# One layer of a hybrid encoder on one core: the residual stage's output product in split passes, with its loads reordered and its transposes moved by one tile

## The reference, cut to what matters

```python
x = layer_norm(x, ln_in_g, ln_in_b)                      # trunk input, once
mix = sigmoid(g_a) * (y_a @ w_up_a) + sigmoid(g_b) * (y_b @ w_up_b)
x = layer_norm(ALPHA * x + (1 + gt1) * (mix @ w_out), ln1_g, ln1_b)
h2 = x * (1 + sc2) + sh2
ffn = hier_moe(h2, w_rg, b_rg, w_re, b_re, w_gate_e, w_up_e, w_down_e)
x = layer_norm(ALPHA * x + (1 + gt2) * ffn, ln2_g, ln2_b)
```

## Time and profile before

| what | value |
| --- | --- |
| median of 3 runs | 2190.09 us (2184.65 to 2190.78) |
| profiled execution, its own time | 2189.32 us |
| its span | 2187.5 us |
| TensorE busy | 1895.8 us, 87% of the span |
| VectorE, ScalarE, GpSimd busy | 949.9, 612.0, 435.6 us |
| mean granted TensorE clock | 0.922 of full speed |
| residual stage, first DMA issue to last instruction | 1600.2 to 1786.3 us, 186 us |

### The profile page before, as it was taken

How to read it: one execution, slowest core, us unless ns; L and a number is a source line. 1 busy time by engine, 2 the same in 40 slices (tenths; PEclk the granted TensorE clock), 3 DMA queues, 4 the chain that set the end, 5 groups by cost and what they waited for, 6 DMA issues and landing times. The chain is left out here.

```text
span 2187.5 us, 28807 instructions
## 1 busy us (share of the span) xinstructions
PE 1895.8 (87%) x10605; PEld 1495.8 (68%) x10606; DVE 949.9 (43%) x2110; ACT 612.0 (28%) x1257; POOL 435.6 (20%) x281
## 2 busy tenths in 40 slices
PE   7797998999999998979997699999977952999990
PEld 2597898989899898968883488888833531444440
DVE  5345756474665757234444111111125661333335
ACT  2543444435353443244443100100000000111114
POOL 0121112111212111111000121212115534222220
PEclk8798999999999999989997799999988975999995
DMA  9110110101011010132107611111052235688765
GB/s 355 53 63 18 35 55 28 57 23 53 32 53 55 20 55 13 34 114 72 36 8 272 238 34 53 38 44 34 24 194 87 87 153 193 218 290 262 217 163 178
DMA packets 61760, 219.24 MB, mean 100 GB/s; under 512 B 8430, under 2 KB 16846, under 8 KB 56534
## 3 DMA queue, kind: packets, MB, share of 16 engines
q1 hardware_dynamic: 53448, 190.03, 24.3%
q0 software_dynamic: 8208, 27.81, 5.2%
HBM read 177.90 MB, written 42.53 MB: 101 GB/s over the span
## 5 line engine op out<-in xcount | busy, mean ns | idle before, releaser
L143 PE MATMUL bk<-hT_high,w_high 128*128 128x352 f32 x840 | 302.4, 360 | 3.9 <-DVE ssq L1194 3.9
L144 PE MATMUL bk<-hT_low,w_high 128*128 128x352 f32 x840 | 278.9, 332 | 0.0
L145 PE MATMUL bk<-hT_high,w_low 128*128 128x352 f32 x840 | 278.4, 331 | 0.0
L2284 PE MATMUL psU<-wgu,xgT 128*128 x400 | 178.4, 599 | 2.0 <-DVE xgT L2350 2.0
L143 PEld LDWEIGHTS bk<-hT_high,w_high 128*128 128x128 f32 x840 | 166.2, 198 | 4.4 <-DVE ssq L1194 4.0
L144 PEld LDWEIGHTS bk<-hT_low,w_high 128*128 128x128 f32 x840 | 165.9, 198 | 0.0
L145 PEld LDWEIGHTS bk<-hT_high,w_low 128*128 128x128 f32 x840 | 164.4, 196 | 0.0
L143 PE MATMUL pm<-hT_high,wg_high 128*128 128x352 f32 x384 | 137.3, 358 | 18.1 <-POOL wg_low L1709 18.1
L780 POOL TENSOR_TENSOR w_low<-wraw,w_high 128x1024 fp32r<-128x1024 f32 x33 | 79.4, 2405 | 354.3 <-ACT w_high L619 183.2
L2284 PEld LDWEIGHTS psU<-wgu,xgT 128*128 128x128 f32 x400 | 76.8, 192 | 98.9 <-issue 98.9
L1864 PE MATMUL py<-wo,mixT 128*128 128x512 f32 (+1 forms) x288 | 128.6, 606 | 13.1 <-DMA wo<-in_w_out 13.1
(11 more groups left out here) (402 smaller groups left out, 3747.4 us busy)
## 6 DMA issues: line engine op xcount, KB each, us to landing
wgu<-in_w_gu SPq DMA_DIRECT2D x16, 2048.0 KB, 8.1
wraw<-in_w_gdn SPq DMA_DIRECT2D x32, 512.0 KB, 3.6
wdn<-in_w_dn SPq DMA_DIRECT2D x16, 1024.0 KB, 12.6
wm<-in_w_mod SPq DMA_DIRECT2D x8, 1024.0 KB, 13.1
tmp_x<-x SPq DMA_DIRECT2D x16, 512.0 KB, 7.4
wg<-in_w_gates SPq DMA_DIRECT2D x16, 512.0 KB, 4.3
wa<-in_w_mod SPq DMA_DIRECT2D x12, 512.0 KB, 5.3
raw<-in_w_mod SPq DMA_DIRECT2D x12, 512.0 KB, 6.6
```

The costliest lines, as they stand in the source:

```text
L143: pe.matmul(out, lh, rh, start=start, stop=False)
L144: pe.matmul(out, lh, rl, start=False, stop=False)
L145: return pe.matmul(out, ll, rh, start=False, stop=stop)
L2284: mm = pe.matmul(psU[b][:, :], xgT[b][:, i, :], c.wgu[:, bass.ds(place, 1), i, :].rearrange("p a c -> p (a c)"), start=(i == 0), stop=(i = ...
```

## The change

`wo` is loaded in 8 pieces of 128 rows (0.5 MB each) through a ring of 3 buffers; ScalarE makes the high part of each piece, VectorE the low part, and the load into a buffer waits for the low part of the piece that it held. The same two engines split each tile of `mixT`. y(t) is three passes per piece and half, all of them F32R, with the piece as the outer loop. In the first tile each piece is waited for alone. The loads behind `wo` stand in another order and have semaphores of their own (`gt_in`, `l0_in`, `l1_in`, `r_in`), and the rows of tile 1 are loaded ahead of the last ones. x1 is not multiplied by ALPHA any more; instead the final stage's epsilon and the experts' gate vectors are divided. `turn` and the copies behind it are done for the tile two before, `route` for the tile three before. The stage has 34 semaphores where it had 24.

```diff
+    WRING, LEADP = 3, 2
-        wo = buf("wo", [P, KD, D])
+        wo = [buf(f"wo{i}", [P, D]) for i in range(WRING)]
+        wo2 = [sb(nc, ctx, f"wo_{n}", [P, KD, D], F32R) for n in ("high", "low")]
+        mix2 = [[sb(nc, ctx, f"mix{i}_{n}", [P, KD, P], F32R) for n in ("high", "low")] for i in range(2)]
...
-                for h in range(2):
-                    sp.dma_start(wo[:, :, h * 512:(h + 1) * 512], d["w_out"][:, :, h * 512:(h + 1) * 512]).then_inc(wo_in[h], 16)
+                def weights(k):
+                    if k >= WRING:
+                        sp.wait_ge(wo_low, k - WRING + 1)
+                    sp.dma_start(wo[k % WRING][:, :], d["w_out"][:, k, :]).then_inc(wo_in[k % WRING], 16)
+
+                for k in range(KD):
+                    weights(k)
                 x_tile(0)
...
+                gates(0)
+                sp.dma_start(l0g[:, :], d["ln_in_g"].partition_broadcast(P)).then_inc(l0_in, 16)
+                sp.dma_start(l0b[:, :], d["ln_in_b"].partition_broadcast(P)).then_inc(l0_in, 16)
+                x_tile(1)
+                sp.dma_start(lng[:, :], d["ln1_g"].partition_broadcast(P)).then_inc(l1_in, 16)
+                sp.dma_start(lnb[:, :], d["ln1_b"].partition_broadcast(P)).then_inc(l1_in, 16)
+                gates(1)
+                gates(2)
+                sp.dma_start(wr[:, :, :], d["w_r"]).then_inc(r_in, 16)
+                sp.dma_start(br[:, :], d["b_r"].partition_broadcast(P)).then_inc(r_in, 16)
...
@@ TensorE
-                    for h in range(2):
-                        if t == 0:
-                            pe.wait_ge(wo_in[h], 16)
-                        for k in range(KD):
-                            mm = pe.matmul(psy[t % 2][0:r, h * 512:(h + 1) * 512], c.mixT[:, k, t * P:t * P + r],
-                                           wo[:, k, h * 512:(h + 1) * 512], start=(k == 0), stop=(k == KD - 1))
+                    pe.wait_ge(mix_low, t + 1)
+                    for k in range(KD):
+                        if t == 0:
+                            pe.wait_ge(wo_low, k + 1)
+                        for h in range(2):
+                            mm = split_matmul(pe, psy[t % 2][0:r, h * 512:(h + 1) * 512], [m[:, k, 0:r] for m in mix2[t % 2]],
+                                              [w[:, k, h * 512:(h + 1) * 512] for w in wo2], start=(k == 0), stop=(k == KD - 1))
                     mm.then_inc(y_ready, 1)
-                    if t >= 2:
-                        route(t - 2)
-                    if t >= 1:
-                        turn(t - 1)
-                route(TILES - 2)
-                turn(TILES - 1)
+                    if t >= LEADP + 1:
+                        route(t - LEADP - 1)
+                    if t >= LEADP:
+                        turn(t - LEADP)
+                for t in range(TILES - LEADP, TILES):
+                    route(t - 1)
+                    turn(t)
                 route(TILES - 1)
@@ ScalarE
+                mix_up(0)
+                for k in range(KD):
+                    act.wait_ge(wo_in[k % WRING], 16 * (k // WRING + 1))
+                    act.activation(wo2[0][:, k, :], wo[k % WRING][:, :], ACT.Copy).then_inc(wo_high, 1)
+                mix_up(1)
...
+                        if t + 2 < TILES:
+                            mix_up(t + 2)
-                    if t >= 1:
-                        u = t - 1
+                    if t >= LEADP:
+                        u = t - LEADP
@@ GpSimd
-                pool.wait_ge(small, 16 * 12)
+                pool.wait_ge(l0_in, 32)
...
+                    if t == 0:
+                        pool.wait_ge(gt_in[1], 32)
+                        pool.wait_ge(gt_in[2], 32)
@@ VectorE
+                def mix_down(t):
...
+                    dve.tensor_tensor(low, c.mixT[:, :, t * P:t * P + r], plain(high), ALU.subtract).then_inc(mix_low, 1)
...
+                mix_down(0)
+                for k in range(KD):
+                    dve.wait_ge(wo_high, k + 1)
+                    dve.tensor_tensor(wo2[1][:, k, :], wo[k % WRING][:, :], plain(wo2[0][:, k, :]), ALU.subtract).then_inc(wo_low, 1)
+                mix_down(1)
-                dve.wait_ge(small, 16 * 12)
-                for m in (lng, lnb):
-                    st.link(dve.tensor_scalar(m[:, :], m[:, :], ALPHA, None, ALU.mult))
-                st.link(dve.tensor_scalar(flat2(gt[:, 1, :, :]), flat2(gt[:, 1, :, :]), 1.0 / ALPHA, None, ALU.mult))
-                for t in range(TILES + 1):
+                dve.wait_ge(gt_in[0], 32)
+                for t in range(TILES + LEADP):
...
                         dve.tensor_tensor(xn[0:r, :], xn[0:r, :], lnb[0:r, :], ALU.add).then_inc(x1_ready, 1)
-                    if t >= 1:
-                        u = t - 1
+                        if t + 2 < TILES:
+                            mix_down(t + 2)
+                    if t >= LEADP:
+                        u = t - LEADP
@@ experts, VectorE
+                dve.tensor_scalar(flat2(gt[:, :, :]), flat2(gt[:, :, :]), 1.0 / ALPHA, None, ALU.mult).then_inc(gt_made, 1)
+                dve.wait_ge(gt_made, 1)
                 dve.tensor_tensor(gt[:, 1, :], gt[:, 1, :], gt[:, 0, :], ALU.subtract).then_inc(gt_made, 1)
@@ final, VectorE
-                dve.memset(eps[:, :], LN_EPS).then_inc(init, 1)
+                dve.memset(eps[:, :], LN_EPS / ALPHA ** 2).then_inc(init, 1)
```

More of the change, by code:

```diff
@@ L1795, in phase_residual @@
         psr = ctx.enter_context(nc.psum_tensor("p_rt", [P, 512], F32))
-        wo_in = [c.sem(f"r_wo{h}") for h in range(2)]
+        wo_in = [c.sem(f"r_wo{i}") for i in range(WRING)]
+        wo_high, wo_low, mix_high, mix_low = (c.sem("r_" + n) for n in ("wohigh", "wolow", "mixhigh", "mixlow"))
         x_in, x_out, h_out = ([c.sem(f"r_{n}{i}") for i in range(2)] for n in ("xin", "xout", "hout"))
-        small, y_ready, var_ready, std_ready, x1_ready, h2_ready, xT, ha, hd, chain, rt, res, init, norm, xg, x_made = (
-            c.sem("r_" + n) for n in ("small", "y", "var", "std", "x1", "h2", "xT", "ha", "hd", "chain", "rt",
+        gt_in = [c.sem(f"r_gt{g}") for g in range(3)]
+        l0_in, l1_in, r_in, y_ready, var_ready, std_ready, x1_ready, h2_ready, xT, ha, hd, chain, rt, res, init, norm, xg, x_made = (
+            c.sem("r_" + n) for n in ("l0", "l1", "rin", "y", "var", "std", "x1", "h2", "xT", "ha", "hd", "chain", "rt",
                                       "res", "init", "norm", "xg", "xmade"))
@@ L1809, in _, with gates @@
+                for k in range(KD):
+                    weights(k)
                 x_tile(0)
                 rows = d["gate_rows"].rearrange("(g s k) c -> g s (k c)", g=4, s=2)
-                for g in range(3):
+                def gates(g):
                     for st in range(2):
-                        sp.dma_start(gt[:, g, st, :], rows[g, st].partition_broadcast(P)).then_inc(small, 16)
-                sp.dma_start(l0g[:, :], d["ln_in_g"].partition_broadcast(P)).then_inc(small, 16)
-                sp.dma_start(l0b[:, :], d["ln_in_b"].partition_broadcast(P)).then_inc(small, 16)
@@ L1816, in _ @@
[L1816 to L1819, removed]
+                        sp.dma_start(gt[:, g, st, :], rows[g, st].partition_broadcast(P)).then_inc(gt_in[g], 16)
+                gates(0)
+                sp.dma_start(l0g[:, :], d["ln_in_g"].partition_broadcast(P)).then_inc(l0_in, 16)
@@ L1849, in route @@
                     pe.wait_ge(hd, t + 1)
-                    pe.wait_ge(small, 16 * 12)
+                    pe.wait_ge(r_in, 32)
                     for k in range(KD):
@@ L1876, in _, with mix_up @@
             def _(act):
+                def mix_up(t):
+                    r = rows_of(t)
+                    if t >= 2:
+                        act.wait_ge(y_ready, t - 1)
+                        act.wait_ge(mix_low, t - 1)
+                    act.activation(mix2[t % 2][0][:, :, 0:r], c.mixT[:, :, t * P:t * P + r], ACT.Copy).then_inc(mix_high, 1)
+                mix_up(0)
[3 more added lines that the diff above has]
+                mix_up(1)
                 act.wait_ge(init, 1)
-                for t in range(TILES + 1):
+                for t in range(TILES + LEADP):
                     if t < TILES:
@@ L1917, in _ @@
                 st = Chain(dve, chain)
-                dve.memset(eps[:, :], LN_EPS).then_inc(init, 1)
-                st.link(dve.memset(c.lg[:, TILES - 1, :], 0.0))
-                dve.wait_ge(small, 16 * 12)
-                for m in (lng, lnb):
-                    st.link(dve.tensor_scalar(m[:, :], m[:, :], ALPHA, None, ALU.mult))
-                st.link(dve.tensor_scalar(flat2(gt[:, 1, :, :]), flat2(gt[:, 1, :, :]), 1.0 / ALPHA, None, ALU.mult))
-                for t in range(TILES + 1):
+                def mix_down(t):
+                    r = rows_of(t)
+                    dve.wait_ge(mix_high, t + 1)
+                    if t >= 2:
+                        dve.wait_ge(y_ready, t - 1)
```

(9 more changed lines are left out.)

8 lines of the change are left out of this document (4 added, 4 removed).

## The result

The changed kernel takes 2174.3 us (median of 6 runs, 2171.0 to 2178.0) against 2190.3 of the kernel before (6 runs): ratio 0.9931, 95% interval 0.9917 to 0.9945, so 12 to 18 us faster by the interval's ends, clear of the 0.3% named in the prediction.

The account below looks back on a forecast made before the run. TensorE was taken to bound the residual stage's middle at 16.35 us per tile, GpSimd's ring next at 15.0. Terms -27.0 (last x1), +4.5 (tail), +1.4 (experts), +0.5 (semaphores) made -20.6 from 2189.3: 2168.7, said as 2169, range 2158 to 2181.

Parts of the forecast that it names:

- GpSimd's ring: Middle tiles: store, load of next rows, then GpSimd's lift and h2; 14.1 us plus lock waits, taken as 15.0 per tile.
- the case priced at 14.8: Middle tiles, after the lift: GpSimd takes the lock first, so only VectorE's residual sum falls between; 14.8 us per tile.
- the prediction's sign: Middle tiles: the gate product is released by its own engine or GpSimd's lift rather than by TensorE.
- e2's theory A: That run's middle tiles: GpSimd's and VectorE's lock holders can't overlap, period falls from 15.0 to 14.2 or 14.5 us.
- the start: Stage's start: l0b lands at 1624.3, first x1 is done at 1637.9; bounds 4 us earlier to 5 later.
- a start that is not 10 us shorter: Stage's start: named as a sign of being wrong; h2(0) was forecast at 1644.6, before 1654.5.
- the tail: Stage's end: six steps of copies, routes and turns behind x1(8) take 12.3 us instead of 7.8, +4.5.
- The scaling in experts: Experts stage: the added scaling of 128x2048 before the first gather costs 1.35 us, ends 0.8 and 3.3, entered as +1.4.
- rival 3: Middle tiles: three passes save nothing, TensorE stays at 16.4 us per tile; total 2185, no change; chance 0.08.
- Rivals 1 and 2: Middle: locks miss each other, period 14.0, total 2163, chance 0.2. Start: loads land out of order, 8 later, 2177, 0.14.
- Rival 4: Residual stage: TensorE's waits in every tile keep its clock at 1.2 GHz, 26.1 us per tile; total 2256, chance 0.07.
- 1.00 from the fifth tile on: Middle tiles: TensorE's granted clock at its full level from there on, named as a sign that would show the prediction.

Follow-up runs that it names:

- e3: Changed kernel with the low part of mixT for tiles 2 to 8 cut to one column per piece; stage 166.7 us against 167.4, ratio 0.9914.
- e2: Changed kernel with the load of the next tile's rows issued ahead of SyncE's wait for h2; stage 165.1 us against 167.4, ratio 0.9910.
- e6: Changed kernel with both copies of transposed h2 earlier in each tile: VectorE's before the residual sum, ScalarE's before the square root; stage 162.7 us, ratio 0.9904.
- e4: Changed kernel with the float32 product back, without split parts or the ring of wo; stage 164.2 us against 167.4, ratio 0.9927.
- e5: Changed kernel with the float32 product back and the transposes one tile earlier; stage 170.3 us against 167.4, ratio 0.9932.
- e1: Changed kernel with turn back to the tile one before and route to two before; stage 173.5 us against 167.4, ratio 0.9963.
- e8: Changed kernel with VectorE and GpSimd again waiting at the start for every load, no scalings put back; stage 178.4 us against 167.4, ratio 0.9982.
- e10: Changed kernel with the float32 product, next rows loaded ahead of the wait for h2, and h2's copies earlier; stage 162.3 us against 167.4, ratio 0.9898.

## Why the prediction was right, and where it was not

**Right in the middle.** The pace went from TensorE to GpSimd's ring as forecast: from x1(0) to x1(8) the trace has 113.7 us, the prediction 113.6 (1637.9 to 1751.5). Most of its terms hold: the wait for the rows 4.3 to 4.9 (4.4), the period 15.0 (15.0), `mix_down` all but free (e3: 0.7 for the whole stage), the pass 0.2266 (0.225). Between the two orders at the lock the 15.0 was partly luck. GpSimd was first, the case priced at 14.8, while the prediction's own terms for it, 4.4 + 9.7 + 1.1, are 15.2; in the trace GpSimd's four instructions took 10.54 us from the first start to the last end, and with the wait that is 15.0. The gate product did wait for TensorE in three tiles (4.00, 0.28 and 0.79 us), against the prediction's sign, but each time ahead of the lock or of the lift, so that the residual sum ended no later for it. e2 shows the next floor where e2's theory A put it, at 14.2. The Trainium skill's page "SBUF — State Buffer", section "Who interferes with whom", says that a VectorE instruction with two SBUF inputs and a GpSimd one that reads SBUF exclude each other and that issue order decides; the trace agrees, with 3.33 and 3.26 us at 1703.87 and 1706.20.

**Mis-sized: the start, by 2.7 us.** Forecast x1(0) at 37.7 us into the stage, measured 40.4. The bound was named rightly, the landing of l0b, but put at 24.1 where it was 25.3, and the residual sum of tile 0 lost the race for the lock (3.33 instead of 1.2), which the prediction had given it. Some of that delay came back behind it. It also missed a wait: y(2) needs `mix_down(2)`, which stands behind x1(0), and waited 8.3 us, then began at the lower clock. That was absorbed: y(2) ended near 1657.7, the lift of tile 2 at 1658.6. The prediction had named as a sign of being wrong a start that is not 10 us shorter. By that sign it was wrong about the start: x1(0) came 8.2 us earlier than before (40.4 for 48.6) and h2(0) 7.2 (47.1 for 54.3), 2.7 later than the "near 1645" forecast for it.

**Mis-sized: the tail, by 1.0.** 13.3 against 12.3, the same six steps; +5.5 instead of +4.5, the upper end, as route(7) ran at the lower clock too (3.57). The prediction had put this down to the place of VectorE's copy of tile 6; e6, which moves this copy and ScalarE's with it, takes the 5.5 away. The clock had fallen to its lower level at 1745, behind a wait of only 0.74 us, a route and a turn, and so ahead of the long wait that the prediction named.

**Elsewhere.** The scaling in experts 1.23 us (1.35), the gap between the stages 3.05 for 2.41, +0.6 (0.5); e4, with 35 semaphores, has 3.11. From the stage's end to the span's end 403.3 us against 401.2: +2.1, forecast +1.9. The remaining 2.1 us by which the profiled stage began later is scatter.

In sum 2168.7 was forecast for the profiled execution, 2174.8 measured: 2.7 start, 1.0 tail, 2.1 scatter, 0.2 elsewhere.

**Wrong: the price of rival 3.** "The three passes save nothing" was priced at 2185, no change. e4, whose TensorE really needs 16.4 per tile, took 2173.4. The step that failed took the pace of 16.4 as binding in all tiles, so that only the start's gain was left. But TensorE at 16.35 had only been bound to the start by its wait for h2(0); freed by the later transposes and the pieces of `wo` it begins 4 us into the stage and is never idle. The right sum was of TensorE's work alone, 139 us, plus 4 at the start and what follows y(8). So the total was right for a partly wrong reason: of the 27.0 us forecast for the stage's body, 10.9 were the start's and 16.1 fell between x1(0) and x1(8) (129.7 before, 113.6 forecast), reckoned at the faster pace per tile; e4, at the old pace, takes 116.9 there and reaches the same total.

**Rivals 1 and 2** did not come: the period was 15.0 and not 14.0, l0b landed 1.2 us later than forecast and not 8, and h2(0) waited for x1(0), not for a gate vector.

**Rival 4** did not come either, but the clock did not stay at 1.00 from the fifth tile on, as the prediction had named as its sign. Two windows over the middle tiles (columns as above), then what happened in them:

```profile
1673.50:1688.30 14.80, 13.54 (x70) 11.33 (x69) 11.13 (x11) 1.73 (x3) 10.36 (x5) 0.96 0.28 106
1688.30:1703.60 15.30, 15.30 (x77) 12.96 (x76) 11.18 (x11) 1.73 (x3) 10.27 (x5) 0.93 0.29 104
...
1684.34 1.93 PE L1867 MATMUL p_rt<-wr,h2T 128*128 128x20 f32 x16 [1.26 <-issue]
1687.46 0.63 PE L144 MATMUL py<-wo_low,mix_high 128*128 128x512 f32 x1
1687.89 0.63 PE L145 MATMUL py<-wo_high,mix_low 128*128 128x512 f32 x1
...
1714.50 1.93 PE L1867 MATMUL p_rt<-wr,h2T 128*128 128x20 f32 x16 [1.26 <-issue]
1717.66 0.39 PE L145 MATMUL py<-wo_high,mix_low 128*128 128x512 f32 x1
1717.89 0.39 PE L143 MATMUL py<-wo_high,mix_high 128*128 128x512 f32 x1
```

TensorE waited 1.26 us ahead of a route in two tiles. Behind the first of these waits the clock was at its lower level from 1687.0 to about 1690.5, with the passes 0.43 us apart; behind the second it stayed up. The lower clock made y(5) some 1.6 us longer. That used up TensorE's wait of the next tile and no more, as the residual sum waited for GpSimd's lift until 1703.8 anyway: the rival failed for the slack, not because such waits leave the clock alone. The Trainium skill's "TensorE: Matmul & The Clock Gate", section "HAM oscillation — how this bites in real kernels", tells of a kernel in which TensorE waits for a load in every tile and starts every tile at the lower level. Here that happened in one of the middle tiles and not in each.

**Open.** Each attribution of 3 us rests on single profiles of the stage; the totals can't tell e4 from the changed kernel (2173.4, 2174.3), nor e5 from e4 (2174.5, 2173.4), though their stages differ by 6.1; that e1 and e8 are slower than the changed kernel the totals do show. With the clock rising as late as in e10, e4's stage would be some 1.3 longer, so the price of 3 for the split may be nearer 2; that is an estimate. How much of the 15.7 is the three scalings was not tried alone. Whether a larger ring of `wo` would give back e4's start was not tried.

## What to carry to other kernels

A faster product buys nothing while another engine's ring (load, two instructions, two more, store, load) stands just below its pace: write down each engine's loop before and after, and the lock's holders as a loop of their own. Ask of each wait on a shared semaphore which load the waiter truly needs; that was the largest part here, and it needs no arithmetic. Moving work later to free an engine is paid for at the end, once; look there for the one instruction that stands behind the last tile's chain.

## What the runs showed of the hardware that was not expected

- TensorE's clock was at its lower level behind a wait of 2.92 us (e1: a turn in 1.97 instead of 1.07, passes 0.43 apart instead of 0.23), and in the changed kernel once behind a wait of 1.26 us and a route, but not behind another of the same length. I had taken 5.8 us as the shortest wait that did this. In e3 it fell once in the middle tiles behind a wait of 1.00 us (from about 1697.3 to 1700.7); in e4, where TensorE never waits there, not at all.
- Split passes of 512 columns cost 0.2266 us each against 0.158 at 352: 0.013 and 0.012 us over one column per 1/2.4 ns, so over these two sizes the overhead is per pass and hardly depends on the columns.
- The gap between the residual stage and the next grew with the stage's semaphores, 2.41 us with 24, 3.05 with 34, 3.11 with 35 (e4): 0.064 us for each.
- VectorE's scaling of 128x2048 took 1.23 us, as much as a product of 128x1024 with two SBUF inputs.
